# First-layer experts of a two-layer mixer: latent and context products swap places in every other weight row block

## What is computed

```
def expert_choice_ffn(h, w_router, w_gate, w_up, w_down):
    ...
    gate, idx = lax.top_k(jnp.swapaxes(aff, 1, 2), cap)
    xs = jax.vmap(lambda hb, ib: hb[ib])(h, idx)
    hid = jax.nn.silu(jnp.einsum('becd,edf->becf', xs, w_gate)) * jnp.einsum('becd,edf->becf', xs, w_up)
    y = jnp.einsum('becf,efd->becd', hid, w_down) * gate[..., None].astype(h.dtype)
    ...
...
h = h + mod_l[5] * expert_choice_ffn(modulate(h, ln2_g[layer], mod_l[3], mod_l[4]), *moe)
if need_ctx:
    ...
    hc = hc + mod_c[5] * expert_choice_ffn(modulate(hc, ln2_g[layer], mod_c[3], mod_c[4]), *moe)
```

## Time and profile before

| | |
|---|---|
| median of 3 runs | 2824.57 us (2821.34 to 2827.41) |
| the profiled execution | 2827.35 us |
| its span, first to last instruction | 2825.1 us |
| experts of layer 0, TensorE | 1104.6 to 1713 us |
| experts of layer 1, TensorE | 2269.5 to about 2792 us |
| TensorE busy with matmuls | 2247.1 us (80% of the span) |
| VectorE, ScalarE, GpSimd busy | 716.6, 408.4, 209.8 us |
| DMA read from memory | 532.87 MB |

### The profile page before, as it was taken

How to read it: one execution, slowest core, us unless ns; L and a number is a source line. 1 busy time by engine, 2 the same in 40 slices (tenths; PEclk the granted TensorE clock), 3 DMA queues, 4 the chain that set the end, 5 groups by cost and what they waited for, 6 DMA issues and landing times.

```text
span 2825.1 us, 29724 instructions
## 1 busy us (share of the span) xinstructions
PE 2247.1 (80%) x11582; PEld 1089.9 (39%) x11582; DVE 716.6 (25%) x1311; ACT 408.4 (14%) x880; POOL 209.8 (7%) x174
## 2 busy tenths in 40 slices
PE   4898999917329785999999995999899577777774
PEld 0543666517229352222222222454696322222221
DVE  0205332365666423111101102010353400000001
ACT  1013221232120110000000002100352100000000
POOL 0000000032231000110001101000000000000000
PEclk8999999956558886999999998999999789999998
DMA  8226431010112233999999995210310289999997
GB/s 310 79 89 209 125 120 38 25 60 31 60 38 73 107 135 132 338 346 351 347 348 345 351 357 173 67 52 0 120 61 16 112 331 400 396 396 396 397 397 260
DMA packets 168727, 564.13 MB, mean 200 GB/s; under 512 B 19696, under 2 KB 32496, under 8 KB 168608
## 3 DMA queue, kind: packets, MB, share of 16 engines
q1 hardware_dynamic: 156864, 522.58, 49.3%
q0 software_dynamic: 10416, 34.58, 4.6%
q10 hardware_dynamic: 1328, 5.24, 0.5%
HBM read 532.87 MB, written 29.46 MB: 199 GB/s over the span
## 4 chain that ended last, share of the span: by engine, by line
PE 65%; DMA 18%; DVE 10%; ACT 2%; issue 2%; SPq 1%; POOL 1%; DVEq 0%; ACTq 0%; POOLq 0%
PE ps L1557 17%; DMA ring_sb<-expert_w_gate 7%; PE ps L1565 6%; PE ps L1365 5%; DMA ring_sb<-expert_w_up 5%; PE ps L440 4%; PE ps L1807 3%; PE ps L736 3%; DMA ring_sb<-expert_w_down 2%; PE ps L625 2%; PE ps L1785 2%; PE ps L1794 2%; PE ps L229 2%; PE ps L1870 2%; DMA ring_sb<-ada_w 2%
## 5 line engine op out<-in xcount | busy, mean ns | idle before, releaser
L1557 PE MATMUL ps<-ring_sb,work_sb 128*64 128x512 f32 x3072 | 752.0, 612 | 162.0 <-DMA ring_sb<-expert_w_gate 81.6
L1557 PEld LDWEIGHTS ps<-ring_sb,work_sb 128*64 128x64 f32 x3072 | 206.8, 138 | 687.4 <-issue 665.9
L1565 PE MATMUL ps<-ring_sb,work_sb 128*32 128x512 f32 x1536 | 205.9, 608 | 0.0
L1665 DVE TENSOR_TENSOR work_sb<-ps,work_sb 128x512 f32<-128x512 f32 x32 | 20.6, 686 | 729.2 <-PE ps L1565 382.1
L1365 PE MATMUL ps<-ring_sb,work_sb 128*128 128x512 f32 x320 | 140.3, 601 | 2.7 <-DVE work_sb L1935 1.9
L229 PE MATMUL ps<-ring_sb,sT_sb 128*32 128x512 f32 x384 | 99.3, 675 | 41.0 <-DMA ring_sb<-ada_w 41.0
L1716 POOL DMA_INDIRECT hl_rows<-work_sb x32 | 45.6, 1425 | 1047.1 <-DVE work_sb L1679 976.7
L1636 ACT ACTIVATE work_sb<-ps 128x1024 f32<-128x1024 f32 x16 | 16.4, 1024 | 685.7 <-PE ps L1565 358.1
L935 PE MATMUL ps<-work_sb 32*32 32x32 f32 x384 | 10.9, 236 | 123.9 <-DVE work_sb L1121 123.9
L440 PE MATMUL ps<-ring_sb,work_sb 128*128 128x512 f32 (+1 forms) x288 | 105.9, 530 | 0.9 <-DVE work_sb L337 0.9
L736 PE MATMUL ps<-work_sb,ring_sb 128*128 128x512 f32 x192 | 98.0, 592 | 0.0
(11 more groups left out here) (317 smaller groups left out, 2703.4 us busy)
## 6 DMA issues: line engine op xcount, KB each, us to landing
ring_sb<-expert_w_gate SPq DMA_DIRECT2D x256, 512.0 KB, 7.2
ring_sb<-expert_w_up SPq DMA_DIRECT2D x256, 512.0 KB, 6.9
ring_sb<-expert_w_down SPq DMA_DIRECT2D x256, 512.0 KB, 5.6
ring_sb<-ada_w SPq DMA_DIRECT2D x96, 512.0 KB, 5.2
ring_sb<-wout SPq DMA_DIRECT2D x16, 512.0 KB, 6.9
work_sb<-bias POOLq DMA_DIRECT2D x16, 512.0 KB, 4.0
ring_sb<-wconv SPq DMA_DIRECT2D x12, 512.0 KB, 3.3
work_sb<-gb_rows SPq DMA_DIRECT2D x12, 512.0 KB, 3.9
```

Source lines behind the costliest of these rows:

```text
L1557: mm = pe.matmul(ps[64 * e:64 * e + 64, bank + n, :], lat_src[:, k, 64 * e:64 * e + 64], us[e][:, n * 512:(n + 1) * 512], start=(k == 0), ...
L1565: mm = pe.matmul(ps[g:g + 32, bank_c, :], ctx_src(k, e), us[e][:, n * 512:(n + 1) * 512], start=(k == 0), stop=(k == KT - 1))
```

## The change

In layer 0's `product` the latent part and the context part become two inner functions. Blocks with an even k do latent then context, as before. Blocks with an odd k do context first and then latent, and there the latent matmuls raise `w_free`. Layer 1 does what it did. No instruction is added or taken away, and each block still waits for its two tiles at its head.

```diff
@@ -1552,20 +1552,31 @@
                         j = u0 + 16 * m + 2 * k + e
                         pe.wait_ge(w_land[j % RING], 16 * (j // RING + 1) + p * (16 * 48 // RING))
                         us.append(ring[:, j % RING, :])
-                    for n in range(2):
-                        for e in range(2):
-                            mm = pe.matmul(ps[64 * e:64 * e + 64, bank + n, :], lat_src[:, k, 64 * e:64 * e + 64],
-                                           us[e][:, n * 512:(n + 1) * 512], start=(k == 0), stop=(k == KT - 1))
-                            if l == 1 and n == 1:
-                                mm.then_inc(w_free, 1)
-                    if l == 0:
+                    def latent(last):
+                        for n in range(2):
+                            for e in range(2):
+                                mm = pe.matmul(ps[64 * e:64 * e + 64, bank + n, :], lat_src[:, k, 64 * e:64 * e + 64],
+                                               us[e][:, n * 512:(n + 1) * 512], start=(k == 0), stop=(k == KT - 1))
+                                if last and n == 1:
+                                    mm.then_inc(w_free, 1)
+
+                    def context(last):
                         for e in range(2):
                             for n in range(2):
                                 g = 32 * (2 * e + n)
                                 mm = pe.matmul(ps[g:g + 32, bank_c, :], ctx_src(k, e), us[e][:, n * 512:(n + 1) * 512],
                                                start=(k == 0), stop=(k == KT - 1))
-                                if n == 1:
+                                if last and n == 1:
                                     mm.then_inc(w_free, 1)
+
+                    if l == 1:
+                        latent(True)
+                    elif k % 2 == 0:
+                        latent(False)
+                        context(True)
+                    else:
+                        context(False)
+                        latent(True)
 
             def rows_c(k, e):
                 return XSC[:, k, 32 * e:32 * e + 32]
```

## The result

| | before | changed |
|---|---|---|
| median of the runs (6 each) | 2825.02 us (2818.96 to 2829.19) | 2809.64 us (2806.97 to 2811.07) |
| the profiled execution | 2827.35 us | 2809.43 us |
| its span | 2825.1 us | 2807.2 us |

The ratio is 0.9947 with a 95% interval of 0.9934 to 0.9960: 15.0 us faster, between 11 and 19. The prediction was 2807.5 us in a range of 2798 to 2817.

A forecast was written before the change was run, and what follows sets the result against it. TensorE was taken to bound layer 0, except for weight waits in the gate product; transfers bound layer 1. Of 25.3 us, 18.6 reach the end, less 1.6 leaves 17.0: from 2824.57 to 2807.5 us, range 2798 to 2817.

The forecast's parts named there:

- The price of a width change: Layer 0's blocks: a change to context and one back cost 0.288 us together, 0.144 us each.
- The rival at 2813.5 us: Joined parts still pay their weight load: 16.6 us saved in all, 11 us reach the end; chance 0.05.
- The count: Layer 0's products: 22 width changes fewer a pair, 3.17 us a pair, 25.3 us for 8 pairs.
- What reaches the end: Up and down products keep 17.3 us; the gate product keeps 1.3 us, in first and last pair; 18.6 us.
- The allowance for a shrunken lead: Behind the gate product's wait, late tiles the old lead hid can show: 0.2 us a pair, 1.6 us in all.
- That the waits do not grow: Rival: layer 0's buffers are freed earlier, so all 25 us come through, 2799.3 us; chance 0.13.
- That the transfers bind the whole stage: Rival: transfers bind more than the gate product; half the gain behind it is lost, 2815.9 us; chance 0.15.
- The clock: Rival: longer waits bring more falls to half clock, 1.65 us each; 2814.2 us or, slower than before, 2825.8; chance 0.04.

The follow-up runs named there:

- tiny_before: Kernel before with 8 rows in each adding and gathering transfer, most tokens and sums left out; 2773.32 us, ratio 0.9810, stage 583.0 us.
- tiny_after: Changed kernel with 8 rows in each adding and gathering transfer, most tokens and sums left out; 2744.70 us, 0.9721 of the kernel before, stage 556.6 us.
- ctx_first: Kernel before with context then latent in every block of layer 0, the number of width changes kept; 2822.47 us, ratio 0.9995.
- updown_only: Changed kernel with the swap undone in the gate product, so only up and down products swap; 2811.67 us, 0.9962 of the kernel before.
- late_before: Kernel before with layer 0's adds of a pair issued after the next pair's up product, gathers behind them; 2815.52 us, ratio 0.9962.
- late_after: Changed kernel with layer 0's adds issued after the next pair's up product, gathers behind them; 2790.23 us, 0.9880 of the kernel before.
- quad: Changed kernel with two blocks of layer 0 joined to a unit, four width changes a product; 2868.93 us, 1.0148 of the kernel before.

## Why the prediction was right

**The price of a width change.** Put at 0.144 us by taking layer 1's latent blocks and the conditioning weights from the block of 2.863 us. tiny_before and tiny_after give 0.144 us with nothing in the way. The 5.44 us, 3.65 us and 1.92 us named ahead of the result are the figures of the trace.

**A joined part pays no bare load.** The rival at 2813.5 us is out: a joined part of 16 records is as long as the sum says, its loads stand at 0.43 us from each other behind the first, and the pair in the tiny kernels is as long as the sum says too. With it falls, for this kernel, the rule of the Trainium skill, TensorE: Matmul & The Clock Gate, Part 3, section The mechanism, that loads overlap running matmuls only where row groups differ; the same section also names a background weight buffer as a way to overlap. All loads here use 128 rows, and within a width they run beside the matmuls (0.14 us each, with no step above 0.43 us).

**The count.** 22 a pair, 176 in all, 25.3 us, was short by 7: the prediction overlooked that down and gate product now join between pairs. 183 changes at 0.144 us are 26.4 us, and the two tiny kernels are 26.4 us of stage apart. The forecast hardly moves by it, since these joins stand at the head of the gate product, whose saving it took as lost in six pairs. ctx_first, with no change in the count, gives 1.4 us, within the noise.

**What reaches the end.** The sum lost the gate product's savings (25.3 to 18.6 us) and 1.6 us more, and came to 17.0. All runs together give 15.0 us. The profiled executions are 17.9 us apart, their stages 17.7; that the two agree so well is chance, for the changed kernel reached the stage 2.8 us later and was 3.4 us shorter in layer 1's experts, which the change leaves alone. In the stage the waits grew by 4.5 us. For gate tiles 13 to 20 waits with 24 to 28 us had been put down, and 14 with 24.2 us were found. The six pairs with waits have a period of 74.64 us on average (from 1179.67 to 1627.52), and 74.5 had been put down. Three places at half clock, as before.

The place of the loss was less sharp than told. I had it that the up and down products keep all they save and the gate product nothing. updown_only kept 10.7 us (7 to 14) of 17.1, where nearly all had been put down, and in its trace the gate product waited more and fell to half clock more often. That shortening the earlier products cuts the lead into the next gate product fits this, but one profile of each kernel cannot tell it from the spread of the waits; I leave it open. The price and the waits for gate tiles were foreseen. That what is lost between them came out right in sum, 8.3 us in the prediction and 8.7 us of stage in the trace, is in part luck.

**The allowance for a shrunken lead** (1.6 us, waits beyond the gate product) was not found where it was put: up and down tiles cost 0.5 us of waits, 0.2 before. Something of its size went elsewhere. Of the 26.4 us saved 17.7 are seen. 4.5 us are waits. 1.5 us are a slower start of the first pair at half clock (its first two blocks take 5.32 and 3.04 us, 4.19 and 2.86 before, with one change fewer). All 15 waits tear a join: 15 x 0.144 = 2.2 us, an estimate. This leaves 0.5 us.

**The other rivals.** That the waits do not grow is out for this kernel, but it is what happens when the adds are moved: late_before to late_after. That the transfers bind the whole stage is out for this kernel, since waits outside the gate product are 0.5 us and tiny_after moves 365 GB/s without one. The clock did not fall more often in the changed kernel than before; in updown_only it did, and that cost it some 5 us.

## What to carry to other kernels

A change between matmuls of 64 and of 32 columns cost 0.144 us here, so put equal widths side by side where the data already lie there, and read the price from a stretch of each width alone. Count the changes over the whole queue, also where one repetition meets the next. Before counting the saving, look where the same engine waits for transfers: there it comes back as a longer wait, and here moving the other traffic by a product and a half was worth 22 us on top of the reordering's 15. A move by two products gave 11 us with the old order and 19 with the new. Joining further must not hold buffers longer than the ring can spare: halving the changes once more cost 57 us.

## What the runs showed of the hardware beyond that

Small indirect transfers beside a stream of 512 KB tiles cost more than the bytes that the trace counts for them. While adds ran (1256 to 1266, kernel before) the queues took (packets, MB, share of the engines):

```profile
q1 hardware_dynamic: 817, 2.95, 76.8%
q0 software_dynamic: 159, 0.39, 23.8%
```

The ring's queue q1 needs 26% of the engines for a MB, that of the adds 61%. Taking the adds down from 64 rows to 8 in each took 12 to 17 us off layer 1, where the bytes left out (16 x 56 rows of 4 KB, 3.7 MB) would take 9 us at that stage's 399 GB/s, and 14 us of waits off layer 0. Whether an add's own reading of the row it adds to makes the difference, no run here shows. And a wait can be dearer than its length: in layer 0 the three kernels with 4.2 us of waits or less had no half clock behind the first blocks, updown_only with 23.4 us had six places, and quad with 75.5 us some 51 us. It is not a fixed price, since late_before had 13.6 us of waits and none, and ctx_first 19.7 us and one place.
